# Gate and branch products of a transformer encoder turned round: tokens as rows, 512 weight columns per product

## The reference

```python
p = rmsnorm(x) @ w_in[l]                 # 1024 -> ... and 3*1024 gate logits
y_a = mla_branch(...)                    # 8 heads, 512 wide
y_b = spatial_gating_branch(...)         # 512 wide
y_c = memory_branch(...)                 # 4 heads over 256 memory rows, 512 wide
yd = einsum('bsnw,nwd->bsnd', stack([y_a, y_b, y_c]), w_br[l])   # 512 -> 1024 each
gates = sigmoid(gate_logits + b_gate[l])
x = x + sum(gates * yd, axis=2) @ w_out[l]
```

## Time and profile before

| | |
|---|---|
| median of three executions | 1684.73 us |
| the profiled execution | 1685.52 us |
| its span, first to last instruction | 1683.4 us |
| PE busy | 1649.7 us, 98% |
| DVE busy | 1279.0 us, 76% |
| ACT busy | 1049.8 us, 62% |
| gate and branch units, layer 0 | 107.9 to 244.1 us of the span |
| experts, layer 1 | from 718 us on |

### The profile page before, as it was taken

How to read it: one execution, slowest core, us unless ns; L and a number is a source line. 1 busy time by engine, 2 the same in 40 slices (tenths; PEclk the granted TensorE clock), 3 DMA queues, 4 the chain that set the end, 5 groups by cost and what they waited for, 6 DMA issues and landing times.

```text
span 1683.4 us, 24382 instructions
## 1 busy us (share of the span) xinstructions
PE 1649.7 (98%) x9224; PEld 1430.4 (85%) x9224; DVE 1279.0 (76%) x1214; ACT 1049.8 (62%) x964; POOL 24.6 (1%) x46
## 2 busy tenths in 40 slices
PE   7999999999999999999999999999999999999997
PEld 6989998999988999888888888888888888888885
DVE  7555576555465656788888988888888888888997
ACT  6535545343363454477777777777777777777774
POOL 1000000000000000020000000000000000000100
PEclk9999999999999999999999999999999999999999
DMA  8633379877373435789999999999999999999994
GB/s 280 203 125 102 125 232 322 286 233 240 109 223 124 128 102 186 251 297 396 385 393 387 359 393 386 355 395 388 361 381 393 362 392 364 385 391 359 391 393 160
DMA packets 252712, 493.95 MB, mean 293 GB/s; under 512 B 8326, under 2 KB 86736, under 8 KB 252640
## 3 DMA queue, kind: packets, MB, share of 16 engines
q1 hardware_dynamic: 247568, 479.23, 79.5%
q10 hardware_dynamic: 3376, 8.39, 1.3%
q0 software_dynamic: 1696, 5.33, 0.8%
HBM read 473.52 MB, written 19.40 MB: 293 GB/s over the span
## 4 chain that ended last, share of the span: by engine, by line
PE 95%; DVE 2%; ACT 1%; DMA 1%; issue 0%; DVEq 0%; SPq 0%; ACTq 0%
PE bank L614 32%; PE bank L1006 24%; PE bank L1039 18%; PE bank L1010 12%; PE bank L604 3%; PE bank L1023 1%; PE bank L847 1%; PE bank L818 1%; PE bank L673 1%; DVE wlo L1628 1%; ACT whi L1265 0%; DMA raw<-in_w_mkv 0%; ACT pbuf L1278 0%; PE bank L800 0%; PE bank L1051 0%
## 5 line engine op out<-in xcount | busy, mean ns | idle before, releaser
L1996 DVE TENSOR_TENSOR wlo<-raw,whi 128x2048 fp32r<-128x2048 f32 x328 | 748.1, 2289 | 108.2 <-ACT whi L1486 108.0
L1486 ACT ACTIVATE whi<-raw 128x2048 fp32r<-128x2048 f32 x328 | 627.7, 1918 | 178.0 <-PE bank L1010 94.0
L1628 DVE TENSOR_TENSOR wlo<-raw,whi 128x2048 fp32r<-128x2048 f32 (+3 forms) x113 | 249.1, 2209 | 190.7 <-ACT whi L1265 190.5
L1006 PE MATMUL bank<-whi,yT_hi 128*128 128x512 f32 x896 | 354.4, 396 | 0.8 <-DVE yT_lo L1964 0.8
L1006 PE MATMUL bank<-whi,yT_lo 128*128 128x512 f32 x896 | 349.3, 390 | 0.0
L1265 ACT ACTIVATE whi<-raw 128x2048 fp32r<-128x2048 f32 (+3 forms) x113 | 208.6, 1850 | 130.0 <-PE bank L614 114.6
L614 PE MATMUL bank<-hT_hi,whi 128*128 128x256 f32 x848 | 243.4, 287 | 0.0
L1010 PE MATMUL bank<-wlo,yT_hi 128*128 128x512 f32 x896 | 240.0, 390 | 0.0
L614 PE MATMUL bank<-hT_hi,wlo 128*128 128x256 f32 x848 | 239.9, 283 | 0.0
L614 PE MATMUL bank<-hT_lo,whi 128*128 128x256 f32 x848 | 239.9, 283 | 0.0
L1010 PEld LDWEIGHTS bank<-wlo,yT_hi 128*128 128x128 f32 x896 | 168.2, 188 | 35.5
(11 more groups left out here) (263 smaller groups left out, 1745.0 us busy)
## 6 DMA issues: line engine op xcount, KB each, us to landing
raw<-in_moe_w SPq DMA_DIRECT2D x336, 1024.0 KB, 7.4
raw<-in_w_in SPq DMA_DIRECT2D x36, 1024.0 KB, 5.3
raw<-in_dense_w SPq DMA_DIRECT2D x30, 1024.0 KB, 6.7
raw<-in_w_br SPq DMA_DIRECT2D x12, 1024.0 KB, 5.1
raw<-in_w_mkv SPq DMA_DIRECT2D x8, 1024.0 KB, 7.7
raw<-in_w_out SPq DMA_DIRECT2D x8, 1024.0 KB, 5.1
rows_by_slot<-qxT SPq DMA_DIRECT2D x15, 512.0 KB, 7.5
y_by_slot<-qxT SPq DMA_DIRECT2D x9, 512.0 KB, 7.9
```

The source lines that it names most:

```text
L1006: nc.tensor.matmul(b[:, :], hselT[a][:, half, tok(k)], w[:, k, :], start=(half + k + a == 0), stop=False)
L1486: nc.scalar.activation(whi[:, (E0 + n) % SPLIT, :], raw[:, n % RAW, :], ACT.Copy).then_inc(hi_ready, 1)
L1628: V.tensor_tensor(wlo[:, m % SPLIT, 0:size], raw[:, pieces[n][1], 0:size], whi[:, m % SPLIT, 0:size].bitcast(F32), ALU.subtract).then_inc( ...
L1996: V.tensor_tensor(wlo[:, s, :], raw[:, n % RAW, :], whi[:, s, :].bitcast(F32), ALU.subtract).then_inc(lo_ready, 1)
```

## The change

Gates and branches are now worked out with the 128 tokens of a row block as the stationary operand and 512 weight columns as the moving one. For each branch n, each half of 512 columns and each row block t there is a gate bank (always bank 6 + t; 24 matmuls, in two pieces of weights k) and a branch bank (12 matmuls). The matmuls of branches 1 and 2 form one stream that is cut into 16 fills of 18: four fills, parts 0 to 3, make one half of a branch. In part 1 the gate of t = 0 is done, in part 2 that of t = 1 and half of branch t = 0, in part 3 the rest.

The bias can no longer be ACT's per-row bias. POOL brings it as a row of 512 broadcast to all partitions (six in a layer), and DVE adds it to the gate out of PSUM (`gate_add`); ACT takes tanh of that in place; DVE multiplies with the branch and sums over branches (`gate_merge`). The sum stands with tokens as rows, so PE transposes it, 16 times in a layer (`transpose_merged`): the first half within the stream of branch 0, the second within the first output product. ACT and DVE split it from PSUM (`merged_high`, `merged_low`). Two bank lists replace the one over six banks: banks 0 to 5 in the memory steps and for `qT`/`kT`, banks 0 to 3 for `as`, `apT`, the branches and the transposed sum. The memory rows of layer 0 are loaded again once the second half has been transposed.

The core of the diff (the removed functions stand above; the new bookkeeping of names, bias-row semaphores and ACT's loops, which mirror DVE's, are left out):

```diff
--- before.py
+++ after.py
+        turn[0] = 0
+        low = (0, 1, 2, 3)
         for step in mixer_steps(heads, x_heads):
-            if step[0] != "O":
-                take((step[0], l) + step[1:])
+            if step[0] == "fill":
+                n, half, part = filled(step[1])
+                if part == 0:
+                    for t in range(2):
+                        take(("gate", l, n, half, t), bank=6 + t)
+                elif part > 1:
+                    take(("br", l, n, half, part - 2), among=low)
+            elif step[0] in ("as", "apT"):
+                take((step[0], l) + step[1:], among=low)
+            elif step[0] != "O":
+                take((step[0], l) + step[1:], among=(0, 1, 2, 3, 4, 5))
...
             take(("o", l, t), bank=4 + t)
         for n in range(2):
-            take(("oT", l, n))
-        for d in range(8):
-            take(("unit", l, 0, d))
-        for n in range(2):
+            take(("oT", l, n), bank=4 + n)
+        for half in range(2):
             for t in range(2):
-                take(("out", l, t, n))
+                take(("gate", l, 0, half, t), bank=6 + t)
+            if half:
+                for n in range(2):
+                    take(("mT", l, n), among=low)
+            for t in range(2):
+                take(("br", l, 0, half, t), among=low)
+        take(("out", l, 0, 0), bank=4)
+        for n in (2, 3):
+            take(("mT", l, n), among=low)
+        take(("out", l, 1, 0), bank=5)
+        turn[0] = 0
+        for t in range(2):
+            take(("out", l, t, 1))
...
+PER_FILL = 18
+def filled(i):
+    return 1 + i // 8, i // 4 % 2, i % 4
...
+        gated_tmp = sgv[:, :].rearrange("p (t c) -> p t c", t=T)
+        gate_rows = [cqkv[:, h, 0:HALF] for h in range(2)] + [pbuf[:, h * HALF:(h + 1) * HALF] for h in range(2)]
...
+                for half in range(2):
+                    c0 = C_GATE + n * D + half * HALF
+                    for k in range(2):
+                        mixer_piece(("gate", l, n, half, k), rows(wi, c0, c0 + HALF, k * hk, (k + 1) * hk))
+                    mixer_piece(("br", l, n, half), rows(w_br[l, n], half * HALF, (half + 1) * HALF))
...
+                def branch(n):
+                    def products(bank, src, w, chunks, start, stop, *names):
+                        for q, (x0, w0) in enumerate(chunks):
+                            for i, (a, b_) in enumerate(((0, 0), (0, 1), (1, 0))):
+                                last = q == len(chunks) - 1 and i == 2
+                                ins = nc.tensor.matmul(bank, src(a, x0), w[b_][:, w0, :], start=(start and q + i == 0),
+                                                       stop=(stop and last))
+                                if last and names:
+                                    mark(ins, *names)
+                                yield ins, bool(last and names)
+                    for half in range(2):
+                        for t in range(T):
+                            claim(("gate", l, n, half, t))
+                        for k in range(2):
+                            w = weight(("gate", l, n, half, k), KD // 2)
+                            for t in range(T):
+                                names = [("gate", l, n, half, t)] if k else []
+                                if t:
+                                    names.append(("piece", "gate", l, n, half, k))
+                                yield from products(banks[groups["gate", l, n, half, t].bank][:, :],
+                                                    lambda a, c: hT[a][:, c, tok(t)], w,
+                                                    [(4 * k + q, q) for q in range(4)], k == 0, k == 1, *names)
+                        if half == 0:
+                            if n == 1:
+                                pe.wait_ge(yb_ready, l + 1)
+                            for i in range(XH if n == 2 else 0):
+                                read(pe, ("mo", l, i))
+                            for i in range(2 if n == 0 else 0):
+                                read(pe, ("oT", l, i))
+                        w = weight(("br", l, n, half), KB)
+                        for t in range(T):
+                            b = claim(("br", l, n, half, t))
+                            names = [("br", l, n, half, t)] + ([("piece", "br", l, n, half)] if t else [])
+                            yield from products(b[:, :], lambda a, c: yT[a][:, n // 2, c, tok(t)], w,
+                                                [(q, q) for q in range(KB)], True, True, *names)
+                def transpose_merged(half):
+                    for t in range(T):
+                        pe.wait_ge(merged, 2 * T * l + T * half + t + 1)
+                        for n in (2 * half, 2 * half + 1):
+                            name = ("mT", l, n)
+                            b = banks[groups[name].bank] if t else claim(name)
+                            for c in range(2):
+                                a = c * SEQ + t * P
+                                ins = nc.tensor.transpose(b[:, a:a + P], hn[:, t, tok(2 * n + c)], ident[:, :])
+                            if t == T - 1:
+                                mark(ins, name)
...
+                flow = itertools.chain(branch(1), branch(2))
                 for step in steps:
                     kind = step[0]
                     name = (kind, l) + step[1:]
-                    if kind == "unit":
-                        unit(*step[1:])
+                    if kind == "fill":
+                        for _ in range(PER_FILL):
+                            ins, marked = next(flow)
+                        if marked:
+                            marks[name] = [count, 0]
+                        else:
+                            mark(ins, name)
...
-                for d in range(KD):
-                    unit(0, d)
+                assert next(flow, None) is None
+                for i, _ in enumerate(branch(0)):
+                    if i == 8 * PER_FILL // 2 + 24 - 1:
+                        transpose_merged(0)
                 for n in range(2):
                     for k in range(2):
-                        if n == 0:
-                            pe.wait_ge(merged, KD * l + KD // 2 * (k + 1))
+                        if n == 0 and k == 0:
+                            for i in (0, 1):
+                                read(pe, ("mT", l, i))
+                        if n == 0 and k == 1:
+                            for i in (2, 3):
+                                read(pe, ("mT", l, i))
...
+                            if n + k == 0 and t:
+                                transpose_merged(1)
...
+            def bring_gate_rows(l):
+                reached(pool, ("cT", l, 2))
+                for half in range(2):
+                    bring_gate_row(l, 1, half)
+                for half in range(2):
+                    read(pool, ("gate", l, 1, half, T - 1))
+                    bring_gate_row(l, 2, half)
+                reached(pool, ("apT", l, H - 1))
+                for half in range(2):
+                    bring_gate_row(l, 0, half)
+            bring_gate_rows(0)
             nc.gpsimd.memset(zeros, 0.0).then_inc(zeros_made, 1)
-            pool.wait_ge(merged, KD)
+            reached(pool, ("mT", 0, 3))
             for t in range(T):
                 pool.dma_start(hn[:, t, :], mem[0, t * P:(t + 1) * P, :]).then_inc(mem_again[t], 16)
+            bring_gate_rows(1)
...
+                def gate_tanh(n, half, t):
+                    read(act, ("gate", l, n, half, t))
+                    nc.scalar.activation(sig[t], sig[t], ACT.Tanh, scale=0.5).then_inc(tanh_ready, 1)
+                def merged_high(n):
+                    b = full(act, ("mT", l, n))
+                    nc.scalar.activation(mT[0][:, 2 * n:2 * n + 2, :].rearrange("p k s -> p (k s)"), b[:, :],
+                                         ACT.Copy).then_inc(merged_hi, 1)
...
+                def gate_add(n, half, t):
+                    b = full(dve, ("gate", l, n, half, t))
+                    i = gate_row(n, half)
+                    dve.wait_ge(gate_row_in[i], gate_row_count(l, n))
+                    free(V.tensor_tensor(sig[t], b[:, :], gate_rows[i], ALU.add), ("gate", l, n, half, t))
+                def gate_merge(n, half, t):
+                    nonlocal gated
+                    name = ("br", l, n, half, t)
+                    gated += 1
+                    dve.wait_ge(tanh_ready, gated)
+                    b = full(dve, name)
+                    total = hn[:, t, half * HALF:(half + 1) * HALF]
+                    dst = total if n == 1 else gated_tmp[:, t, :]
+                    free(V.scalar_tensor_tensor(out=dst, in0=sig[t], scalar=1.0, in1=b[:, :], op0=ALU.add,
                                                 op1=ALU.mult), name)
+                    read(dve, name)
+                    if n == 2:
+                        link(V.tensor_tensor(total, total, dst, ALU.add))
```

(30 more changed lines are left out.)

123 lines of the change are left out of this document (37 added, 86 removed).

## The result

The changed kernel takes **1693.55 us** in the median of four runs (1692.45 to 1694.67), the kernel before 1684.64 us (1684.5 to 1684.79): 8.9 us slower by the medians; the ratio on record is 1.0049 with a 95% interval of 1.0037 to 1.0062, where the two medians' own quotient is 1.0053. Forecast were 1688.7 us and a range of 1683 to 1693 us. The sign is right; the median is 0.55 us above the range and 4.9 us above the forecast (by the ratio of 1.0049 on 1684.73 us it would be 1693.0 us, at the edge of the range).

The account below looks back on a forecast made before the run. PE's stream, busy 98% of the span, was taken to bound the kernel. Terms -11.4 + 4.0 + 11.6 - 1.9 + 0.4 = +2.7 us gave 1687.4; plus 1.6 for the clock, rounded down, 1688.7 us, range 1683 to 1693.

Parts of the forecast that it names:

- The wait: PE waiting for DVE's merge of t = 0 before branch 1's t = 1 product: 5.5 us per layer.
- TensorE's clock: Behind the wait PE may fall to 1.2 GHz, costing 1.6 us each time; charged once of two.
- The products: Gate and branch matmuls of 512 columns instead of 256: -5.7 us per layer, -11.4 us in all.
- The transposes: 16 added PE transposes per layer, with changes between fp32 and fp32r work: +4.0 us in all.
- The end of the memory steps: PE's waits at k transposes and first scores shrink from 2.05 to 1.1 us per layer: -1.9 us in all.
- First latent scores: In layer 0 they start at 150.7 us against 147.67, about 3 us later than before.
- The margins: Spare time of 0.3 to 0.7 us in latent steps and at the transposed sum hides DVE's work: charged 0.
- The 0.4 us at the transposes of `o`: At the end of the steps PE waits 0.2 us per layer for DVE: +0.4 us.
- Rival 1: The wait on the merge is there but PE's clock holds: 1687.4 us; chance 0.26.
- Rival 2: The wait on the merge is hidden or far shorter, DVE being earlier: 1675.8 us; chance 0.13.
- Rival 3: More waits, in the latent steps and output product, 4 x 0.7 us per layer: 1693 us; chance 0.10.
- Rival 4: Products of 512 columns run at 0.240 us, so nothing is saved: 1698.8 us; chance 0.03.

Follow-up runs that it names:

- experiment 1: Changed kernel with only the bank plan altered: branch product of t = 1 to bank 4, third and fourth `mo` to banks 5 and 2; 1678.44 us.
- experiment 2: Changed kernel, bank kept, with DVE merging t = 0 right behind the fourth memory step's maximum; 1682.10 us.
- experiment 6: Changed kernel with each gate and branch matmul of 512 columns done as two of 256; 1699.99 us.
- experiment 9: Changed kernel with 10 more unread filler matmuls in layer 1's router stage; 1692.43 us.
- experiment 4: Changed kernel with 20 unread matmuls of 128 columns filling PE's wait on the merge; 1688.60 us.
- experiment 8: Kernel of experiment 1 with 10 more unread filler matmuls in layer 1's router stage; 1677.62 us.
- experiment 10: Kernel of experiment 8 with 16 unread matmuls ahead of the first transposes; 1675.65 us.
- experiment 3: Changed kernel with 40 unread matmuls of 128 columns in PE's wait on the merge; 1693.90 us.
- experiment 5: Changed kernel with 10 unread matmuls in PE's wait on the merge, leaving 2.6 us idle per layer; 1688.82 us.
- experiment 7: Kernel of experiment 1 with each of the 16 transposes of the gated sum per layer done twice; 1680.21 us.

## Why the prediction was right in its sign and short in its size

**The wait.** One per layer, at the place, behind the operation and for the reason that was followed: 4.8 us where 5.5 was worked out, near 128 and 568 us. PE arrives 19.8 us behind the first fill instead of 19.6, the merge ends about 24.5 us behind it instead of 25.1. The prices of 0.69 us for adds and merge were right. Experiments 1 and 2 show the cause from both sides.

**TensorE's clock: the step that failed.** It was charged 1.6 us once of two, because the only row for it was the start. It falls in both layers, at all six waits of the three traces that have them (the changed kernel, experiments 6 and 9); of the other runs of the changed kernel only the mean clock is known, 0.993 or 0.994. Behind the wait it stays low until 138.4 and 575.3 us, which costs 2.2 and 1.3 us there and 2.7 us net at the end (experiment 4). The price of one fall was about right (1.6 us taken; 1.3 us measured for a low stretch of 3.4 us, 2.2 and, in layer 1 of experiment 9, 2.8 for one of 6.8); what was wrong is that one of two was charged, 1.3 us in the sum where 2.7 came, and that no fall was reckoned with in any other stage. With the next two paragraphs the lower clock is 1.4 + 2.9 + 1.2 us of what the forecast lacked. The Trainium skill, "TensorE: Matmul & The Clock Gate", section "HAM oscillation — how this bites in real kernels", describes just this: a wait between groups of matmuls lets the clock drop, and the next group pays for it at its start. The traces agree: 0.42 us per matmul behind 4.8 us of wait, 0.23 behind 0.35 us of it.

**The router stage: missing in the prediction.** 2.9 us of the 8.9 are there. Its steps are the same as before, and the earlier part of the kernel decides only when they come. No row of the kernel before shows it, as its own trace is one of those without the stretch; whether other executions of that kernel have it is open. The same page of the Trainium skill, section "A second HAM failure mode: psum-queue depth-cycling", says that many short idle times between groups of matmuls are enough for the clock to go down and up; experiments 8 and 9, where the clock was 1.00 with gaps of 0.5 to 0.7 us filled, fit that and do not prove it.

**The start: chance.** 1.2 of the 8.9 us are ahead of the first fill. In the traces without experiment 10's the first maximum of the scores comes either at 100.4 to 101.1 us (before, experiments 1, 3, 5, 6) or at 102.0 to 102.5 us (the changed kernel, 2, 4, 7, 8, 9). The first group is the one whose granted clock rises at 13.8 to 14.8 us, the second that where it rises at 18.6 to 19.6 us. The change touches nothing there, so that the changed kernel's trace is of the second group and the kernel before's of the first is luck. Without this and the router stage the loss would be about 4.8 us, 1689.4 us, close to the forecast; but that too is in part luck, since errors of both signs follow.

**The products.** -11.4 us predicted, -10.7 as PE's work and -8.4 net (experiment 6): per fill 0.19 us, not 0.23, and not all of it on the path. This is the largest single term that was mis-sized, by 3.0 us. The first step of a fill, from fp32 to fp32r work, is 0.32 us for 512 columns (166.85 to 167.17) and was counted at 0.2265. **The transposes**: +4.0 predicted; experiment 7's second set cost 2.6 net for 3.5 of work, so the first set's 4.0 may be some 3. **The end of the memory steps**: -1.9 predicted, -1.5 measured (4.0 to 2.5 us). First latent scores: +6.6 us in layer 0 (154.29 against 147.67); less 1.2 of the start and 2.2 of the clock it is 3.3, where 3 was predicted. **The margins** of 0.3 to 0.7 us in the latent steps and at the transposed sum held, and the bias rows and the memory rows were never waited for; PE's wait for the normalised rows even fell from 2.8 to 1.0 us in all.

**The sum with measured net terms**: products -8.4; transposes +2.9 (4.0 x 2.6 / 3.5); the waits on the merge +11.0 (experiment 4 against 8, spans of 1686.9 and 1676.2 us and 0.3 us of start); clock in the layers +2.7; router stage +2.9; start +1.2; end of the memory steps -1.5; the wait for the normalised rows from 2.8 to the 1.8 us of experiment 4 -1.0. The 0.4 us at the transposes of `o` did not come. That is +9.8 against +8.9: 0.9 us are not placed; the terms may overlap in the waits.

**The rivals.** Rival 1 (1687.4, clock holds) is what experiment 4 built: 1688.6 us. Rival 2 (1675.8, no wait) is what experiments 1 and 8 built: 1678.4 and 1677.6 us. Rivals 3 and 4 did not occur.

## What to carry to other kernels

When a bank plan deals out buffers by turn, follow each new draw to its previous user and ask where that user's release stands in a strictly ordered engine: here one bank shared by two row blocks stands between a gain of 6 us and a loss of 9 (13.5 us of it in the layers). Count a wait of several microseconds on TensorE as the wait plus what the work behind it pays at the lower clock, and where such a wait can't be avoided, idle matmuls into a free bank buy the clock back, 2.7 us here (experiment 4). Before a difference is charged to a change, look at the stages that it doesn't touch: nearly half of this one (2.9 + 1.2 of 8.9 us) lay there.

## What the runs showed of the hardware that was not expected

- An idle time of TensorE of 4.8 to 4.9 us brought the granted clock to 0.50 in all three traces that had it, twice in each, for 3.4 or 6.8 us; one of 1.2 us did in neither layer of its trace (experiment 2), nor did one of 2.6 us (experiment 5).
- The clock also fell, in four of nine traces of the same steps, in a stage with no wait over 0.7 us ahead of the fall. With three more pieces of filler of 0.7 to 0.9 us it was 1.00 in all three traces.
- At the start the lower level lasted until 13.8 to 14.8 us in some traces and until 18.6 to 19.6 us in others, of kernels with the same start; by the first maximum of the scores it is worth about 1.6 us (102.0 to 102.5 us against 100.4 to 101.1), which is part of why runs of one kernel differ.
- A matmul of fp32 operands with 128 columns is two records and 0.22 us (experiment 3: from the filler's start at 127.06 to the next matmul's at 135.91 us, 8.85 / 40), twice a transpose's 0.11 us.
